# A two-layer hybrid decoder step: f16 sample products stacked over 96 rows, chunk states before exponent differences, weights split first and steps one to three places on in the retention groups

## The chip, the cores and the metric

One core of a Trainium2 chip runs the whole program. The metric is the device time of one execution in microseconds. Times are the median of three timed runs; the rows below come from one further execution that the hardware profiler recorded.

## The reference

One inference step of a decoder of two layers, for a prompt of 16 + 512 tokens and, with the same weights, for eight running sequences of four new tokens each (32 sample tokens). Every layer mixes tokens by four HGRN2 heads and four retention heads of 128 x 128 state, then runs a convolutional FFN. What bears on the change is the state update of a head, here for HGRN2 (retention is alike, with fixed decays):

```python
s_new = exp(b_last)[..., None] * s0 + einsum('bshk,bshv->bhkv', k * exp(b_last[:, None] - b), v)
```

For each sample sequence it is the old state, decayed, plus a product over its four tokens of decayed keys and values. The states of all eight sequences and of the prompt are outputs.

## The kernel before, in words

All arithmetic is f32 in effect. The large products use weights and activations split into an f16 high and an f16 low part (WH, WL, XH, XL): per 128 rows of the contraction six TensorE instructions, three products on two halves of 280 of the 560 tokens (`products`, L510). Smaller products run on f32 operands directly, where each is issued as two instructions.

A layer's mixer is nine stages. **Group** g (0 to 7) computes the four projection tiles of one head (forget gate or key, query, value, output gate; 0 to 3 HGRN, 4 to 7 retention), while TensorE also does the mixing of the head of the group before. A group has 4 tiles of 8 k-steps, 32 k-steps, and the mixing work is written into them by hand: the lists HG_SLOTS, HG_SLOTS_RT and RT_SLOTS give, for each piece of it, the k-step before which it is issued. Group 0 has no mixing work beside it; groups 1 to 3 carry HGRN heads by HG_SLOTS, group 4 the last one by HG_SLOTS_RT, groups 5 to 7 retention heads by RT_SLOTS, and the output projection the last retention head (there the slot numbers are halved, since it holds two tiles' columns of 7 k-steps). Tiles go to two accumulators in PSUM in turn: tiles 0 and 2 to accumulator 0, tiles 1 and 3 to accumulator 1, so k-step 16 needs tile 0 read out (`acc_read[0]`) and k-step 24 tile 1 (`acc_read[1]`). A scratch area SCR has two banks. Each job on a bank waits until the job before it was read (`scr_read`).

Each engine runs its own program in order, with semaphores between them.

- VectorE in an HGRN group: the score masks of the head before (`hg_scores`, L1302 on), the low half of the weight split for slot 1 (`split_lo`, L1153), the gate (`hg_gate`, L1202 to L1212, ending with a scan), the exponent differences (`hg_exponents`, L1217 to L1224), the chunk states of the head before (`hg_states`, L1342, L1347), the output gate, the keys and queries (`hg_query`), the sample states (L1300).
- VectorE in a retention group: the scores (`rt_a`, L1391), the split of slot 1, the key's rotation (L1258 to L1262), the sample states, the split of slot 0, the query's rotation, the norm of the outputs.
- ScalarE copies transposed keys and values out of SCR (`hg_a` L910 to L919, `rt_a` L960 to L970), takes the exponentials (L885 to L891), reads Q, V and G out of the accumulators (`read_acc`, L866) and does the high half of the weight split (`split_hi`, L830). In groups 1 to 3 it reads Q right behind the exponentials.
- GpSimd (POOL) spreads the sample values into VX (32 rows by 8 sequences by 128, zero where the row is another sequence's; L417), decays the old HGRN states (L423), and issues the DMAs of the states.
- SyncE issues the loads of the weights into the two halves of `stage`.

The sample products (`sample_steps`, L624) multiply the decayed keys KVTS[:, 0] by VX: two products of 32 rows by 512 columns in f32 per head, 16 heads in all.

```python
mm(SCR[:, bank, :], KVTS[:, 0, :], VX[:, 4 * n:4 * n + 4, :].rearrange("p b v -> p (b v)"), ...)   # L624
pe.wait_ge(acc_read[c], 1 + l * ACC_TILES + half_tile)          # gemm_tile, ahead of k-steps 0, 8, 16, 24
HG_SLOTS = ([1, 2, 3, 4, 5], [7, 8, 9, 10], [12, 13], [22, 22], [23, 23, 24, 24, 25, 25], [28, 28])
RT_SLOTS = ([4, 5, 6], [6, 7, 8, 9, 10], [12], [12, 13], [15, 16], [21, 22], [29])
```

The parts of RT_SLOTS are: transposes of keys, of values and of the rest; five score products; the final state; the two sample products; two output products (the second with the sample outputs, L632); two centring products; the variance. Those of HG_SLOTS are scores, transposes, chunk states, sample products, outputs, mean squares.

## Time and profile before

| | us |
|---|---|
| median of three timed runs (1738.65 to 1740.34) | 1739.92 |
| the profiled execution's own time | 1742.57 |
| its span, first to last instruction | 1741.0 |
| TensorE busy in it | 1567.8 (90%) |
| VectorE busy | 904.5 (52%) |
| ScalarE busy | 654.0 (38%) |
| GpSimd busy | 154.3 (9%) |
| mean granted TensorE clock | 0.931 of full speed |

The span holds two alike layers. In the first, groups 0 to 7 run from about 49 to 378 us, the output projection and a norm to 494, the FFN to 866; the second follows some 843 us later. The page's busy shares are means over stages of different limits, so the stage, and in it the wait that ends last, is what to look at. "L" and a number is a line of the kernel; an entry such as `[2.45 <-DVE shared L1347]` gives the idle time ahead of an instruction and what ended it.

### The profile page before, as it was taken

To read this page: it belongs to the slowest core of one execution; us is meant where nothing else is said; L and a number is where in the kernel's file an instruction comes from. 1 tells how busy PE (TensorE), PEld (TensorE's weight loads), DVE (VectorE), ACT (ScalarE), POOL (GpSimd) and SP (SyncE) were. 2 spreads that over 40 slices of the span, in tenths; PEclk is the share of its full clock that TensorE was granted. 3 is DMA by queue.
4 is the path that set the end of the run, shared out by engine and by line. 5 is a ranking of instruction groups with operands and counts; after the bars stand their busy time and mean duration, and the time that the engine had idled before them with its cause. 6 is when DMAs were issued, how large, how long until landed. Compare 5 with 4: busy or idle time off the path is not lost.

```text
span 1741.0 us, 31399 instructions
## 1 busy us (share of the span) xinstructions
PE 1567.8 (90%) x12107; PEld 1251.0 (72%) x12107; DVE 904.5 (52%) x1389; ACT 654.0 (38%) x920; POOL 154.3 (9%) x126
## 2 busy tenths in 40 slices
PE   4699999989699999999867999999886999999994
PEld 3477777767578888788755777777765888887883
DVE  4766644444565555533266665444356555553334
ACT  3645523332353334422155452333225443333213
POOL 2111111100200000000030111000002000000002
PEclk8799989988899999999978899999888999999997
DMA  6132222221123332233221224232031223322321
GB/s 192 46 90 77 75 75 75 74 74 55 57 73 97 96 96 77 70 93 95 82 66 51 74 74 111 57 88 78 27 97 48 88 83 96 96 81 74 97 66 51
DMA packets 175035, 138.05 MB, mean 79 GB/s; under 512 B 5064, under 2 KB 169192, under 8 KB 174776
## 3 DMA queue, kind: packets, MB, share of 16 engines
q1 hardware_dynamic: 168192, 113.46, 22.0%
q0 software_dynamic: 5408, 18.60, 3.8%
q10 hardware_dynamic: 1372, 5.16, 0.9%
q8 instruction: 40, 0.66, 0.2%
q14 instruction: 23, 0.19, 0.0%
HBM read 125.12 MB, written 12.07 MB: 79 GB/s over the span
## 4 chain that ended last, share of the span: by engine, by line
PE 77%; DVE 9%; ACT 6%; issue 4%; DVEq 2%; ACTq 1%; DMA 1%; SPq 0%
PE ACC L510 61%; PE SCR L624 2%; PE OT L632 2%; PE SCR L662 1%; ACT WH L830 1%; DVE X L1193 1%; PE OT L684 1%; PE SCR L545 1%; PE SCR L727 1%; DVE Z L1222 1%; DVE Fb L1206 1%; DVE WL L1153 1%; PE OT L600 1%; DVEq L1261 1%; PE OT L599 1%
## 5 line engine op out<-in xcount | busy, mean ns | idle before, releaser
L510 PE MATMUL ACC<-XH,WH 128*128 128x280 f16 x2432 | 502.6, 289 | 70.8 <-DVE XL L1196 43.1
L510 PE MATMUL ACC<-XL,WH 128*128 128x280 f16 x2432 | 502.4, 289 | 0.0
L510 PE MATMUL ACC<-XH,WL 128*128 128x280 f16 x2432 | 501.6, 289 | 0.0
L510 PEld LDWEIGHTS ACC<-XH,WH 128*128 128x128 f16 x2432 | 238.7, 101 | 153.0 <-DVE XL L1196 45.6
L1153 DVE SCALAR_TENSOR_TENSOR WL<-stage,WH 128x2048 f16<-128x2048 f32 (+1 forms) x116 | 245.9, 2120 | 182.0 <-ACT WH L830 170.2
L510 PEld LDWEIGHTS ACC<-XL,WH 128*128 128x128 f16 x2432 | 243.3, 100 | 58.6
L510 PEld LDWEIGHTS ACC<-XH,WL 128*128 128x128 f16 x2432 | 243.3, 100 | 58.0
L830 ACT ACTIVATE WH<-stage 128x2048 f16<-128x2048 f32 (+1 forms) x116 | 204.8, 1766 | 103.7 <-PE ACC L510 86.9
L510 PE MATMUL ACC<-shared,WH 128*128 128x280 f16 x1408 | 225.2, 283 | 0.2
L510 PEld LDWEIGHTS ACC<-shared,WH 128*128 128x128 f16 x1408 | 137.6, 98 | 30.8 <-issue 0.8
L510 PE MATMUL ACC<-shared,WL 128*128 128x280 f16 x704 | 141.5, 283 | 0.0
L408 POOL TENSOR_TENSOR X<-X,T 128x560 f32<-128x560 f32 x40 | 65.2, 1663 | 429.1 <-ACT T L842 429.1
L837 ACT ACTIVATE E<-X 128x560 f32 (+1 forms) x32 | 21.5, 671 | 195.5 <-DVEq L1175 195.5
L510 PE MATMUL ACC<-OHL,WH 128*128 128x280 f16 x512 | 89.0, 300 | 6.0 <-DVE X L1173 6.0
L1173 DVE SCALAR_TENSOR_TENSOR X<-ACC,X 128x560 f32 (+1 forms) x32 | 23.7, 740 | 112.1 <-PE ACC L510 111.4
L510 PEld LDWEIGHTS ACC<-shared,WL 128*128 128x128 f16 x704 | 68.9, 98 | 14.9
L1093 ACT ACTIVATE T<-ACC 128x560 f32<-128x560 f32 x44 | 28.0, 637 | 135.9 <-PE ACC L510 135.5
L510 PEld LDWEIGHTS ACC<-OHL,WH 128*128 128x128 f16 x512 | 52.3, 104 | 23.4 <-DVE X L1173 7.0
L1565 DVE SCALAR_TENSOR_TENSOR Fb<-ACC,Fb 128x560 f32<-128x560 f32 x22 | 16.3, 742 | 92.0 <-PE ACC L510 92.0
L417 POOL TENSOR_TENSOR VX<-KVTS,tab 32x1024 f32<-32x1024 f32 x16 | 30.2, 1886 | 285.4 <-ACTq L920 197.5
L510 PE MATMUL ACC<-OHL,WL 128*128 128x280 f16 x256 | 55.3, 300 | 0.0
L1548 DVE COPY AS<-T 128x32 f32<-128x32 f32 x44 | 8.0, 182 | 90.0 <-ACTq L1096 89.6
(238 smaller groups left out, 1791.4 us busy)
## 6 DMA issues: line engine op xcount, KB each, us to landing
stage<-in_w_in_dram SPq DMA_DIRECT2D x64, 512.0 KB, 5.3
stage<-in_w_a_dram SPq DMA_DIRECT2D x44, 512.0 KB, 4.3
stage<-in_w_b_dram SPq DMA_DIRECT2D x44, 512.0 KB, 4.8
stage<-in_w_down_dram SPq DMA_DIRECT2D x32, 384.0 KB, 3.3
stage<-in_w_down_dram SPq DMA_DIRECT2D x32, 320.0 KB, 3.7
out_dram<-shared POOLq DMA_DIRECT2D x16, 512.0 KB, 3.9
stage<-in_w_o_dram SPq DMA_DIRECT2D x16, 512.0 KB, 3.9
shared<-in_state_hgrn_dram POOLq DMA_DIRECT2D x8, 512.0 KB, 5.7
```

Source lines behind the costliest of these rows:

```text
L408: nc.gpsimd.tensor_tensor(X[:, m, :], X[:, m, :], MU[:, 0:T], ALU.subtract).then_inc(ln_sub, 1)
L417: nc.gpsimd.tensor_tensor(VX[:, :, :], KVTS[:, 1:2, :].to_broadcast([TS, DEC_BATCH, P]), bcast(seqm[0:TS, :], P), ALU.mult).then_inc(vx_re ...
L510: last = mm(ACC[:, acc, h, 0:HALF], lhs, x[:, xk + k, h * HALF:(h + 1) * HALF], start=begin, stop=end)
L545: last = mm(SCR[0:left.shape[1], bank, c * C // 2:(c + 1) * C // 2], left, right, start=True, stop=True)
L599: mm(o, SC[:, (c - 1) * P:c * P], QD[:, t:t + C], start=True, stop=False)
L624: mm(SCR[:, bank, :], KVTS[:, 0, :], VX[:, 4 * n:4 * n + 4, :].rearrange("p b v -> p (b v)"), start=True, stop=True).then_inc(scr_full, 1)
L632: last = mm(OT[:, 1, TP - SPLIT + DEC_SEQ * b:TP - SPLIT + DEC_SEQ * (b + 1)], S0b[:, b, :], qs[:, TP + DEC_SEQ * b:TP + DEC_SEQ * (b + 1) ...
L830: f(WH[:, s, 0:width], stage[:, s, 0:width], ACT.Copy, scale=W_SCALE).then_inc(w_hi[s], 1)
L837: f(SQT[:, 0:T], src, ACT.Square).then_inc(sq_ready, 1)
L1093: f(halves(AX[c][:, 2:2 + T]), ACC[:, c, :, 0:HALF], ACT.Copy, scale=INV_W)
L1153: stt(out=WL[:, s, 0:width], in0=stage[:, s, 0:width], scalar=W_SCALE, in1=WH[:, s, 0:width], op0=ALU.mult, op1=ALU.subtract).then_inc(w_l ...
L1173: stt(out=halves(row(m)), in0=ACC[:, c, :, 0:HALF], scalar=INV_W / ALPHA, in1=halves(row(m)), op0=ALU.mult, op1=ALU.add).then_inc(acc_read ...
```

## The change

- The sample products become one f16 product over 96 rows: keys high, high and low (KV3[:, 0], rows 0-31, 32-63, 64-95) against values high, low and high (KV3[:, 1]). The sample transposes take 96 columns, so that each block arrives in its rows; the columns are copied twice more behind K and V (`twice`). ScalarE writes all 96 rows in f16 as high parts, then a copy of the values in f32 (VTS) for the sample outputs. VectorE (`low_sample_rows`) subtracts to get the two low blocks, and only then releases SCR bank 0. POOL's VX has 96 rows in f16 and waits for the low rows (`kv_low`) instead of the copies.
- In HGRN groups VectorE runs the chunk states (`b`) ahead of the exponent differences, and the low rows behind the gate's readout.
- In retention groups (where `c` is given) VectorE does the split of slot 1 ahead of the scores; the low rows stand behind the first score job.
- RT_SLOTS moves pieces one to three k-steps on.

```diff
         AX, CX = (T1, T2), (T3, Fb)
-        VX = sb("VX", [TS, DEC_BATCH, P])
-        KVTS = sb("KVTS", [TS, 2, P])
+        VX = sb("VX", [TS3, DEC_BATCH, P], F16)
+        KV3 = sb("KV3", [TS3, 2, P], F16)
+        VTS = sb("VTS", [TS, P])
         PTS = sb("PTS", [C, TP])
...
         Fb, T1, T2, T3, B, Q, QS, QD, KE, E, V, G = (
-            sb(n, [P, T + 2]) for n in ("Fb", "T1", "T2", "T3", "B", "Q", "QS", "QD", "KE", "E", "V", "G"))
+            sb(n, [P, T + (2 * TS if n in ("KE", "V") else 2)]) for n in ("Fb", "T1", "T2", "T3", "B", "Q", "QS", "QD", "KE", "E", "V", "G"))
         at = [0]
...
         tok_ready, vx_ready, pts_ready, states_ready = sem("tok_ready"), sem("vx_ready"), sem("pts_ready"), sem("states_ready")
+        kv_high, kv_low = sem("kv_high"), sem("kv_low")
         decays_used = sem("decays_used")
...
             return ap.unsqueeze(2).to_broadcast([ap.shape[0], ap.shape[1], n])
+
+        def twice(t):
+
+            return t[:, T:T + 2 * TS].rearrange("p (a t) -> p a t", a=2)
...
-                pool.wait_ge(tok_ready, hh + 1)
-                nc.gpsimd.tensor_tensor(VX[:, :, :], KVTS[:, 1:2, :].to_broadcast([TS, DEC_BATCH, P]), bcast(seqm[0:TS, :], P),
+                pool.wait_ge(kv_low, hh + 1)
+                nc.gpsimd.tensor_tensor(VX[:, :, :], KV3[:, 1:2, :].to_broadcast([TS3, DEC_BATCH, P]), bcast(seqm[0:TS3, :], P),
                                         ALU.mult).then_inc(vx_ready, 1)
...
                         for i, src in enumerate(sources):
-                            last = nc.tensor.transpose(SCR[0:TS, bank, i * P:(i + 1) * P], src[:, TP:T], ident)
+                            last = nc.tensor.transpose(SCR[0:TS3, bank, i * P:(i + 1) * P], src[:, TP:TP + TS3], ident)
                     last.then_inc(scr_full, 1)
...
                 job(scr, bank)
-                mm(SCR[:, bank, :], KVTS[:, 0, :], VX[:, 4 * n:4 * n + 4, :].rearrange("p b v -> p (b v)"),
+                mm(SCR[:, bank, :], KV3[:, 0, :], VX[:, 4 * n:4 * n + 4, :].rearrange("p b v -> p (b v)"),
                    start=True, stop=True).then_inc(scr_full, 1)
...
                 cols_ = OT[:, 1, TP - SPLIT:REST]
-                mm(cols_, KVTS[:, 1, :], PTSS[:, :], start=True, stop=False, skip_group_check=True)
+                mm(cols_, VTS[:, :], PTSS[:, :], start=True, stop=False, skip_group_check=True)
                 for b in range(DEC_BATCH):
...
                 act.wait_ge(acc_full, 1 + tile + 1)
-                f(halves(buf[:, 0:T]), ACC[:, c, :, 0:HALF], ACT.Copy, scale=INV_W).then_inc(acc_read[c], 1)
+                last = f(halves(buf[:, 0:T]), ACC[:, c, :, 0:HALF], ACT.Copy, scale=INV_W)
+                if buf is V:
+                    last = f(twice(V), ACC[:, c, 1:2, HALF - TS:HALF].to_broadcast([P, 2, TS]), ACT.Copy, scale=INV_W)
+                last.then_inc(acc_read[c], 1)
                 if done is not None:
...
                 act.wait_ge(scr_full, full)
-                f(KVTS[:, :, :], SCR[0:TS, 0, 0:2 * P].rearrange("p (n v) -> p n v", n=2), ACT.Copy).then_inc(scr_read[0], 1)
+                f(KV3[:, :, :], SCR[0:TS3, 0, 0:2 * P].rearrange("p (n v) -> p n v", n=2), ACT.Copy)
+                f(VTS[:, :], SCR[0:TS, 0, P:2 * P], ACT.Copy).then_inc(kv_high, 1)
                 act.drain().then_inc(tok_ready, 1)
...
                 f(VTOK[0:TAIL, 4 * P:5 * P], SCR[0:TAIL, 0, P:2 * P], ACT.Copy)
-                f(KVTS[:, 0, :], SCR[0:TS, 0, 2 * P:3 * P], ACT.Copy, scale=tab[0:TS, ds(cols["k_dec_s"][0] + p, 1)])
-                f(KVTS[:, 1, :], SCR[0:TS, 0, 3 * P:4 * P], ACT.Copy).then_inc(scr_read[0], 1)
+                f(KV3[:, 0, :], SCR[0:TS3, 0, 2 * P:3 * P], ACT.Copy, scale=tab[0:TS3, ds(cols["k_dec_s"][0] + p, 1)])
+                f(KV3[:, 1, :], SCR[0:TS3, 0, 3 * P:4 * P], ACT.Copy)
+                f(VTS[:, :], SCR[0:TS, 0, 3 * P:4 * P], ACT.Copy).then_inc(kv_high, 1)
                 act.drain().then_inc(tok_ready, 1)
...
-            def hg_gate(l, p, tile):
+            def low_sample_rows(hh, at, decay):
+
+                keys, values = (slice(2 * TS, TS3), KV3[2 * TS:TS3, 0, :]), (slice(TS, 2 * TS), KV3[TS:2 * TS, 1, :])
+                dve.wait_ge(kv_high, hh + 1)
+                if decay is None:
+                    tt(keys[1], SCR[keys[0], 0, at:at + P], keys[1], ALU.subtract)
+                else:
+                    stt(out=keys[1], in0=SCR[keys[0], 0, at:at + P], scalar=tab[keys[0], ds(cols["k_dec_s"][0] + decay, 1)],
+                        in1=keys[1], op0=ALU.mult, op1=ALU.subtract)
+                tt(values[1], SCR[values[0], 0, at + P:at + 2 * P], values[1], ALU.subtract).then_inc(scr_read[0], 1)
+                dve.drain().then_inc(kv_low, 1)
+
+            def hg_gate(l, p, tile, low_rows=None):
                 n = l * HEADS + p
...
                 dve.drain().then_inc(f_ready, 1)
+                if low_rows is not None:
+                    low_rows()
...
                 tt(QD[:, 0:T], Q[:, 0:T], E[:, 0:T], ALU.mult)
+                nc.vector.tensor_copy(twice(KE), KE[:, TP:T].unsqueeze(1).to_broadcast([P, 2, TS]))
                 dve.drain().then_inc(ew_ready, 1)
...
                 for job in RT_JOBS:
+                    if job is RT_JOBS[1]:
+                        low_sample_rows(hh, 2 * P, p)
                     full, _ = scr.job(bank)
...
                 hh = l * 2 * HEADS + kind * HEADS + head
-                if a is not None:
+                if c is not None:
+                    split_lo(1, j)
                     a()
-                split_lo(1, j)
+                else:
+                    if a is not None:
+                        a()
+                    split_lo(1, j)
+                hgrn_rows = (lambda: low_sample_rows(hh - 1, 0, None)) if steps else None
                 if kind == 0:
-                    hg_gate(l, head, tile)
-                    hg_exponents(l, head)
+                    hg_gate(l, head, tile, hgrn_rows)
                     if b is not None:
                         b()
+                    hg_exponents(l, head)
                     if d is not None:
...
+                        hgrn_rows()
                         dve.wait_ge(tok_ready, hh)
...
-RT_SLOTS = ([4, 5, 6], [6, 7, 8, 9, 10], [12], [12, 13], [15, 16], [21, 22], [29])
+RT_SLOTS = ([5, 6, 9], [9, 10, 11, 12, 13], [14], [15, 16], [17, 18], [23, 24], [30])
```

## Rows read from the trace of the kernel before

**Rows 1.** The page, part 4: shares of the chain that ended last.

```profile
PE 77%; DVE 9%; ACT 6%; issue 4%; DVEq 2%; ACTq 1%; DMA 1%; SPq 0%
```

**Rows 2.** Table of stretches, group 2: engines' busy us (count), PEclk, DMA.

```profile
135.00:177.00 42.00, 39.55 (x327) 32.84 (x324) 28.79 (x52) 22.68 (x39) 6.14 (x5) 0.96 0.28 76
```

**Rows 3.** Table of waits, TensorE: us in total, times, longest.

```profile
PE SCR L624 <- DVE shared L1347: 17.7, 8, 2.5
...
PE SCR L653 <- ACT shared L960: 16.4, 6, 4.5
```

**Rows 4.** Timeline of TensorE, group 2: start, us, operation.

```profile
150.84 0.40 PE L510 MATMUL ACC<-XH,WL 128*128 128x280 f16 x2
...
153.69 2.05 PE L624 MATMUL SCR<-VX,KVTS 32*128 32x512 f32 x4 [2.45 <-DVE shared L1347]
...
159.20 0.55 PE L599 MATMUL OT<-QD,shared 128*128 128x88 f32 x2
...
170.82 0.69 PE L545 MATMUL SCR<-Z 128*44 128x44 f32 x12
```

**Rows 5.** Timeline of VectorE, group 2.

```profile
144.01 2.19 DVE L1206 TENSOR_TENSOR Fb<-Fb,T 128x560 f32<-128x560 f32 x1 [3.93 <-ACT T L877]
...
146.13 0.73 DVE L1207 TENSOR_TENSOR T<-T 128x560 f32<-128x560 f32 x1
...
148.87 0.71 DVE L1217 TENSOR_TENSOR T<-B 128x528 f32<-128x528 f32 x1
...
152.08 0.28 DVE L1342 COPY shared<-SCR 128x128 f32<-128x128 f32 x1
...
154.96 0.74 DVE L1284 TENSOR_TENSOR G<-G,shared 128x560 f32<-128x560 f32 x1 [0.40 <-issue]
```

**Rows 6.** Timeline of ScalarE, group 2.

```profile
152.19 0.67 ACT L885 ACTIVATE T<-T 128x560 f32<-128x560 f32 x1 [4.37 <-DVE DK L1224]
...
155.84 0.61 ACT L866 ACTIVATE Q<-ACC 128x560 f32<-128x560 f32 x1
```

**Rows 7.** Groups by form, ScalarE: busy, mean ns, idle before.

```profile
L970 ACT ACTIVATE KVTS<-SCR 32x128 f32<-32x128 f32 x8 | 2.0, 249 | 0.0
```

**Rows 8.** Timeline of GpSimd (POOL), group 2.

```profile
141.85 1.89 POOL L417 TENSOR_TENSOR VX<-KVTS,tab 32x1024 f32<-32x1024 f32 x1 [17.15 <-ACTq L920]
...
143.70 1.90 POOL L423 TENSOR_TENSOR shared<-shared,E 128x1024 f32<-128x1024 f32 x1
```

**Rows 9.** Timeline of VectorE in the norm stage of layer 0.

```profile
471.61 5.01 DVE L1193 TENSOR_TENSOR X<-X,QS 128x560 f32<-128x560 f32 x3 [1.78 <-ACT QS L848]
```

**Rows 10.** Table of stretches with the clock; PEclk third from the end.

```profile
302.50:306.00 3.50, 3.48 (x22) 2.47 (x23) 0.86 (x2) 1.38 (x5) 1.70 (x1) 1.00 0.00 0
...
344.00:347.25 3.25, 3.25 (x12) 1.98 (x12) 0.43 (x1) 0.92 (x4) 1.89 (x1) 0.50 0.00 0
...
385.00:391.75 6.75, 5.39 (x16) 3.26 (x17) 1.61 (x3) 2.58 (x10) 1.89 (x1) 0.50 0.01 2
...
951.50:961.75 10.25, 10.25 (x42) 7.50 (x42) 7.94 (x16) 6.00 (x9) 0.74 (x2) 0.50 0.02 7
```

**Rows 11.** Timeline of TensorE, retention groups 5 and 6.

```profile
280.44 0.40 PE L510 MATMUL ACC<-XH,WH 128*128 128x280 f16 x2
...
288.14 0.41 PE L510 MATMUL ACC<-XH,WH 128*128 128x280 f16 x2 [0.88 <-DVE T L1260]
...
302.52 0.28 PE L653 MATMUL SCR<-tab,KE 128*16 128x128 f32 x1 [1.86 <-ACT shared L960]
```

**Rows 12.** Timeline of TensorE, group 1 of both layers.

```profile
110.90 3.00 PE L624 MATMUL SCR<-VX,KVTS 32*128 32x512 f32 x4 [2.47 <-DVE shared L1347]
...
117.82 0.57 PE L599 MATMUL OT<-QD,shared 128*128 128x88 f32 x2
...
950.49 2.96 PE L624 MATMUL SCR<-VX,KVTS 32*128 32x512 f32 x4 [2.46 <-DVE shared L1347]
...
957.37 0.57 PE L599 MATMUL OT<-QD,shared 128*128 128x88 f32 x2
```

More of the change, by code:

```diff
@@ L46 @@
 T = TP + TS
+TS3 = 3 * TS
 HALF = T // 2
@@ L143, in const_tables @@
     put("mask32", causal)
-    put("seq", tok[:, None] // DEC_SEQ == np.arange(DEC_BATCH)[None, :])
+    put("seq", np.tile(tok[:, None] // DEC_SEQ == np.arange(DEC_BATCH)[None, :], (3, 1)))
     log_g = np.log1p(-np.exp2(-5.0 - np.arange(HEADS)))
@@ L154, in const_tables @@
     put("k_dec", np.where(left >= 0, np.exp(np.maximum(left, 0) * log_g[None, None, :]), 0.0) * root)
-    put("k_dec_s", np.exp((DEC_SEQ - 1 - tok % DEC_SEQ)[:, None] * log_g[None, :]) * root)
+    put("k_dec_s", np.tile(np.exp((DEC_SEQ - 1 - tok % DEC_SEQ)[:, None] * log_g[None, :]) * root, (3, 1)))
     put("gamma4", np.broadcast_to(np.exp(DEC_SEQ * log_g), (P, HEADS)))
@@ L653, in rest_transposes @@
                         nc.tensor.transpose(SCR[0:TAIL, 0, n * P:(n + 1) * P], src[:, 4 * P:TP], ident)
-                        last = nc.tensor.transpose(SCR[0:TS, 0, (2 + n) * P:(3 + n) * P], src[:, TP:T], ident)
+                        last = nc.tensor.transpose(SCR[0:TS3, 0, (2 + n) * P:(3 + n) * P], src[:, TP:TP + TS3], ident)
                     last.then_inc(scr_full, 1)
@@ L1275, in rt_query @@
                 tt(QS[:, TP:T], QD[:, TP:T], tab[:, ds(cols["q_dec"][0] + p * TS, TS)], ALU.mult)
+                nc.vector.tensor_copy(twice(KE), KE[:, TP:T].unsqueeze(1).to_broadcast([P, 2, TS]))
                 dve.drain().then_inc(ew_ready, 1)
```

## Prediction

> **What bounds the kernel now.** I read the page first: of the span of 1741.0 us the chain that ended last is 77% TensorE, 9% VectorE and 6% ScalarE [rows 1]. Then the table of stretches, to see where TensorE is not busy: in a group of a linear-recurrence (HGRN) head it is busy 39.55 of 42 us [rows 2]. So such a stage is TensorE's own work plus waits, and the table of waits names them: the sample products behind VectorE's chunk states (L624 on L1347, 17.7 us, eight times), the retention rest transposes behind ScalarE's copies (L653 on L960, 16.4 us, six times, the longest 4.5) [rows 3]; the second tile of a retention pair waits behind the rotation, L1260. Last I laid the four engines' timelines of one group side by side. The FFN stretches and the norms are not touched, and I leave them as they are.
>
> In all that follows a group has 32 k-steps, 0 to 31, each of six weight products. Group 2 of layer 0 stands for groups 1 to 3. A full-clock step is 0.715 us (three pairs, each about 0.24 after the one before, as the last pair starts at 150.84) [rows 4].
>
> **HGRN groups 1 to 3: before.** TensorE finishes step 21 at 151.24, waits 2.45 us, runs the four instructions of the two sample products in 2.05, and comes to step 24 at 159.20. The next group's step 0 is at 170.1, 0.72 before the level products at 170.82: 10.9 us after step 24 [rows 4]. VectorE ends its scan at 148.87, spends 3.21 on the exponent differences (to 152.08) and 2.88 on the chunk states (to 154.96) [rows 5]. ScalarE takes the exponentials at 152.19 and reads Q out of accumulator 1 by 156.45, 4.26 later [rows 6]. Step 24 writes accumulator 1, so it needs that readout; now it is ready 2.75 before it is asked for.
>
> **What the stacked product gives.** 32x512 f32 runs as two instructions per product, about 0.5 us each in the pace of the four; in f16 it is one instruction of 512 columns. The weight products go 280 columns in 0.12 us, so 512 cost an estimated 0.22, two of them 0.44, and 1.6 are saved per head. Bounds: nothing saved, or 1.99 less two LDWEIGHTS-bound issues of 0.1, which is 1.8.
>
> **Where it goes in groups 1 to 3.** The states now run ahead of the differences, so the wait of 2.45 goes too: bank 1 is free 1.55 us into the states, bank 0 2.49 us in. With a scan end of 149.6 (below) TensorE has both products done by about 152.4, steps 22 and 23 and the first two outputs by 154.7. But the 2.88 of states now stand ahead of the differences, and every item behind them shifts: differences, ScalarE's exponentials, Q's readout at 156.45 + 2.88 = 159.33. So step 24 waits for Q for some 5 us and starts when it did before (159.20). Both gains, 4 us a group, become a new wait.
>
> **Delay d of the scan.** The new f32 sample copy on ScalarE, 0.25 [rows 7], and two small VectorE operations (0.2 each, near the 0.28 of the 128-wide copy at 152.08 [rows 5]) put VX on POOL at about 142.6 instead of 141.85. VX and the state decay then hold POOL to 146.4 instead of 145.60 [rows 8]. L1206 took 2.19 where L1207 of equal shape took 0.73, and ended 0.6 after POOL did [rows 5, 8]; in the norm stage three VectorE operations beside POOL's took 5.01, one per POOL operation [rows 9]. So of L1206 and L1207 one now waits behind VX and one behind the decay, and L1207 ends near 147.6 instead of 146.86: d = 0.75. POOL's two rows, on 32 and on 128 partitions, agree at 1.89 and 1.90 us for 1024 elements [rows 8], so 96 partitions cost no more; there is no row for f16 on POOL. Half that time gives d = 0, one and a half times gives 1.6; I take the row's own. The Trainium skill (GPSIMD Engine Reference, section 3.1) counts about 2.6 cycles of 1.2 GHz per element for two inputs and names no type; by it VX is an estimated 2.2 us, d 1.05, and the sum 2 us higher. The row says 1.89.
>
> **Clock after the new wait.** After the wait of 4.5 the granted clock stood at 0.50 from 385.0 to 391.75, with 5.4 us of TensorE's work in it; in group 1 of layer 1 it was 0.50 for 10.25; after a wait of 1.86 it stayed at 1.00 [rows 10, 11]. TensorE's two levels, 2.4 and 1.2 GHz: work at the lower takes twice as long. I charge 4 us of half clock behind a 5.4 us wait, a loss of 2.0, bounds 0 and 3.4. The Trainium skill (TensorE: Matmul & The Clock Gate, part 1) says that the throttled state is the default and that activity releases it, and counts half of the throttled time as lost; by it alone the 5.4 us behind the wait of 4.5 would be charged, 2.7, and the sum 4 higher. The trace agrees that long waits are followed by 0.50.
>
> Groups 2 and 3 of both layers: 0.9 (readout at 160.08 for 159.20) + 2.0 = 2.9, four times, 11.6. By their sample products (110.90 and 950.49 for 153.69) group 1 lies 42.8 earlier in layer 0 and 796.8 later in layer 1, so its readout falls on 117.3 and 956.9 where step 24 stood at 117.82 and 957.37: -0.5 each. From there to the next group were 11.1 and, as the low clock ran on [rows 10], 14.5; 10.8 + 2.0 takes their place, +1.7 and -1.7 [rows 12]. Together 11.6 + 1.2 - 2.2 = **+10.6**.
>
> **Group 4** (last HGRN head beside the first retention tiles). Its order of states and key doesn't change. The key starts 0.7 later (sample copy and low rows), L1262 falls behind POOL, the states are some 0.75 late, so is the first sample product; the products then save 0.8 and 1.6 (half clock in part), and half a microsecond to 1 of half clock lies in steps that start earlier. Step 24 there follows the rotation, which follows the last output product, so this passes through: -2.2 (bounds -0.9 and -2.7), two layers, **-4.4**.
>
> **Retention groups 5 to 7.** The loop there: output products end (280.44), ScalarE copies them and splits slot 0, VectorE splits the rest and rotates, step 24 starts at 288.14: 7.70 [rows 11]. Nothing in it changes. The end of the outputs, counted from step 0, moves by two steps (1.43), by -1.7 for the products, and by 0.7 for a new wait: bank 0 is now released by VectorE's low rows, which wait for ScalarE's KV3 and VTS copies, and the second score product needs bank 0. That is +0.4 in group 5. In groups 6 and 7 the wait of 1.86 shrinks to 0.6, because the rest transposes come at step 9: -0.9 each, and group 7 loses its stretch of half clock from 344.0 to 347.25 [rows 10], -1.5. The second centre product moves behind the rotation, 0.26 in each. Together -2.1 a layer. Against it: between outputs and step 24 now lie five steps and one centre product, 4 us, instead of eight steps, so TensorE waits 2.95 for 0.88. I charge 1.0 of clock per group (bounds 0 and 1.7). Net +0.9 a layer, **+1.8**. VectorE's earlier split of slot 1 costs nothing: ScalarE's half is done 1.9 us after it begins either way, TensorE wants it at step 16, and SP's next load only starts earlier. Behind the low rows on VectorE stand the scores of the later jobs and the key rotation; the key is due at step 16 and has 0.7 to spare. POOL's VX, queued on the low rows, ends 3 us ahead of step 15.
>
> **Output projection.** The wait of 4.5 stays [rows 3], since variance (step 30) and the KTOK copies move with it; the products give 1.5, the bank wait takes 0.6, clock about as before: -0.7, twice, **-1.4**. The copies of K's and V's sample columns (0.2 each on VectorE and ScalarE) lie in gaps of 0.9 and more before the key and the variance; without that cover they cost 0.2 per head, 3 us in all.
>
> **Sum.** 10.6 - 4.4 + 1.8 - 1.4 = +6.6 on the profiled execution's 1742.57, or 1749.2; that execution is 2.65 above the median of 1739.92, so the timed runs should give 1746.5; I say 1746.
>
> **Rivals.**
> (a) The clock stays up: the falls in groups 1 to 3 came after products on 32 rows, which go, and one wait of 1.86 left it at 1.00 [rows 10]. Then 2.0 x 6 and 1.0 x 6 are not paid: 6.6 - 18 = -11.4, 1728, faster. It decides from there on whether the granted clock behind step 24 reads 1.00. Against it stands the wait of 4.5. Chance 0.25.
> (b) POOL is slower on f16 rows: VX at twice 1.89 puts d at 2.65, 1.9 more in six groups, +11.4: 1758. No row speaks for it but that none is f16. Chance 0.12.
> (c) The stacked product doesn't do what it says, and runs as long as f32: the ten heads outside groups 1 to 3 lose 1.6 each, 1762. The f16 pace of the weight products speaks against it. Chance 0.03.
> (d) VX is short (d = 0) and the clock loss is 1.0 instead of 2.0: 6.6 - 0.75 x 6 - 6 = -3.9 for both, 1736, and about 1741 where only one holds: no change. Chance 0.10.
> The forecast has 0.50, with its own 1738 to 1755.
>
> **How the numbers follow.** The range 1729 to 1759 reaches into (a) and (b). About 0.2% (3.5 us) is what a measurement can tell from no change. Faster: (a) and a little of the forecast's low end, 0.27; same: (d) and the end of the forecast near 1743, 0.18; slower: the rest, 0.55.
>
> **What would show it.** Right: in groups 1 to 3 no wait of L624 on L1347 but one of L510 on ScalarE's readout of Q, about 5 us; differences behind the states; L1206 and L1207 both long; PE clock 0.50 behind step 24; in retention groups the wait on L1260 near 3 us, the one on L960 small, a new one on the low rows near 0.7. Wrong: a group period of 39 us or less in groups 1 to 3, or Q read before TensorE asks.

## The result: slower, and the profile of the changed kernel

The changed kernel takes 1766.02 us (1765.23 to 1769.53) beside 1740.13 for the kernel before: a ratio of 1.0153, 95% interval 1.0135 to 1.0171. The forecast was 1746 with a range of 1729 to 1759, so the sign was right and the size was not: +6.6 was summed, +25.9 measured. The profiled execution took 1766.46 us with a span of 1764.9 (before: 1742.57 and 1741.0), and its mean granted clock is 0.921 for 0.931.

Stage lengths, each read from the first level products or first retention transpose of one group to those of the next. In groups 5 to 7 the transposes stand one step later in the changed kernel; its 0.715 us is taken out of group 4 and put to group 7 (in the output projection, with its halved slot numbers, they stand where they stood). The last row reaches to the next layer's first level products, or to the end:

| us, changed less before | forecast, layer 0 / 1 | measured, layer 0 / 1 |
|---|---|---|
| HGRN group 1 | +1.2 / -2.2 | +3.4 / 0.0 |
| HGRN group 2 | +2.9 / +2.9 | +7.1 / +7.1 |
| HGRN group 3 | +2.9 / +2.9 | +6.9 / +6.9 |
| group 4 | -2.2 / -2.2 | -1.5 / -1.5 |
| retention groups 5 to 7 | +0.9 / +0.9 | +1.6 / +1.5 |
| output projection and what follows | -0.7 / -0.7 | -3.7 / -3.8 |

The miss lies in groups 1 to 3. Group 1 of layer 1 took 46.9 us in both kernels; its first level products, in the kernel before and in the changed one, are these:

```profile
925.63 1.11 PE L545 MATMUL SCR<-Z 128*44 128x44 f32 x12
...
939.26 1.11 PE L552 MATMUL SCR<-Z 128*44 128x44 f32 x12
```

The waits of TensorE in the changed kernel (us in total, times, longest) answer to [rows 3]:

```profile
PE OT L606 <- ACT Q L873: 34.0, 6, 5.9
...
PE SCR L702 <- DVE T L1287: 13.9, 6, 2.9
PE SCR L660 <- ACT shared L971: 10.7, 6, 4.5
...
PE SCR L631 <- DVE shared L1375: 9.3, 14, 2.3
...
PE SCR L669 <- DVE KV L1220: 4.9, 6, 0.9
```

The first is the wait that the forecast named, at step 24 for ScalarE's readout of Q (the products' line 510 is now 517 and the outputs' 599 is 606). The second and the last are the forecast's waits behind the rotation (2.95 put down; 2.9 here in groups 5 and 6, some 1.2 in group 7) and behind the low rows (0.7 put down, 0.9 here). The waits for the sample products and the rest transposes shrank.

TensorE in group 2 of layer 0 (start, us, operation, idle before and what ended it), beside [rows 4]:

```profile
154.72 0.39 PE L631 MATMUL SCR<-VX,KV 96*128 96x512 f16 x1 [0.23 <-DVE shared L1375]
155.65 0.39 PE L631 MATMUL SCR<-VX,KV 96*128 96x512 f16 x1 [0.54 <-DVE shared L1375]
...
157.71 0.40 PE L517 MATMUL ACC<-XH,WL 128*128 128x280 f16 x2
163.66 0.73 PE L606 MATMUL OT<-QD,shared 128*128 128x88 f32 x2 [5.55 <-ACT Q L873]
...
169.20 3.58 PE L639 MATMUL OT<-QD,shared 128*128 128x4 f32 x16
...
176.59 1.11 PE L616 MATMUL SCR<-shared,tab 128*128 128x264 f32 x4
...
181.20 0.69 PE L552 MATMUL SCR<-Z 128*44 128x44 f32 x12
```

The two sample products fell from 2.05 us for both to 0.39 each, and their wait from 2.45 to 0.23 and 0.54. Then TensorE stands for 5.55, and from there to the next level products it takes 17.54 us where it took 11.62 [rows 4]. The table of stretches shows the clock over that time (busy time and count of PE, PEld, DVE, ACT, POOL; then the granted clock, third from the end; the ends of a stretch were read on a grid of 0.25 us; compare [rows 2, 10]):

```profile
132.90:181.20 48.30, 41.97 (x315) 35.09 (x314) 29.59 (x53) 22.30 (x41) 6.14 (x5) 0.86 0.31 84
157.50:162.75 5.25, 0.61 (x6) 0.26 (x3) 2.47 (x4) 3.40 (x10) 0.00 (x0) 1.00 0.04 12
162.75:176.50 13.75, 12.84 (x58) 10.87 (x59) 9.58 (x17) 6.46 (x11) 1.78 (x2) 0.50 0.20 52
176.50:181.20 4.70, 4.70 (x37) 3.60 (x34) 1.61 (x3) 1.81 (x4) 0.00 (x0) 1.00 1.06 293
```

For 13.75 us TensorE ran at the lower of its two levels, 1.2 GHz, though it was busy for 12.84 of them. Group 3, and both groups in layer 1, have the same stretch; group 1 has two shorter ones (115.0 to 121.75 and 125.25 to 128.5 in layer 0) behind a wait of 5.9.

VectorE, ScalarE and POOL in the same group, beside [rows 5, 6, 8]:

```profile
147.41 2.82 DVE L1232 TENSOR_TENSOR Fb<-Fb,T 128x560 f32<-128x560 f32 x1 [1.67 <-ACT T L887]
150.16 0.73 DVE L1233 TENSOR_TENSOR T<-T 128x560 f32<-128x560 f32 x1
...
156.03 0.71 DVE L1243 TENSOR_TENSOR T<-B 128x528 f32<-128x528 f32 x1 [0.44 <-issue]
...
163.64 0.45 DVE L1257 TENSOR_SCALAR T<-Q 128x560 f32<-128x560 f32 x1 [3.67 <-ACT Q L873]
```

```profile
159.35 0.67 ACT L895 ACTIVATE T<-T 128x560 f32<-128x560 f32 x1 [7.50 <-DVE DK L1250]
...
162.99 0.61 ACT L873 ACTIVATE Q<-ACC 128x560 f32<-128x560 f32 x1
```

```profile
145.88 1.89 POOL L424 TENSOR_TENSOR VX<-KV,tab 96x1024 f16<-96x1024 f16 x1 [17.69 <-DVEq L1221]
```

The group began 3.24 us later than in the kernel before (132.88 for 129.64). Less that, L1233 ends at 147.65 for 146.86, so the delay d is 0.79 where 0.75 was put down, and Q is ready at 160.36 where 160.08 was. POOL's f16 product on 96 partitions takes the 1.89 us of the f32 one on 32.

### The profile page after: what moved, and what is told of

It is laid out like the page before. It is cut to its first block, busy times and chain, and to the rows that moved or that the text cites. A ratio compares the mean times of both kernels' runs of the same rounds, so it can differ in the third digit from the quotient of the medians.

```text
span 1764.9 us, 31445 instructions
## 1 busy us (share of the span) xinstructions
PE 1557.0 (88%) x12075; PEld 1255.1 (71%) x12075; DVE 918.9 (52%) x1437; ACT 658.0 (37%) x952; POOL 154.3 (9%) x126
## 4 chain that ended last, share of the span: by engine, by line
PE 73%; DVE 10%; ACT 8%; issue 4%; DVEq 3%; ACTq 1%; DMA 1%; SPq 0%
PE ACC L517 60%; PE OT L639 2%; ACT WH L837 2%; DVE X L1205 1%; PE OT L691 1%; PE SCR L669 1%; PE SCR L552 1%; DVEq L1288 1%; DVE Fb L1232 1%; ACT Z L899 1%; DVE Z L1248 1%; DVE WL L1165 1%; PE OT L606 1%; DVE shared L1375 1%; PE SCR L734 1%
## 5 line engine op out<-in xcount | busy, mean ns | idle before, releaser
L517 PE MATMUL ACC<-XH,WH 128*128 128x280 f16 x2432 | 506.0, 291 | 67.5 <-DVE XL L1208 42.2
L517 PEld LDWEIGHTS ACC<-XH,WH 128*128 128x128 f16 x2432 | 241.8, 102 | 135.6 <-DVE XL L1208 45.4
L517 PEld LDWEIGHTS ACC<-shared,WL 128*128 128x128 f16 x704 | 68.9, 98 | 15.1
L424 POOL TENSOR_TENSOR VX<-KV,tab 96x1024 f16<-96x1024 f16 x16 | 30.2, 1887 | 313.3 <-DVEq L1221 313.3
```

The lines of the kernel that those rows point to most:

```text
L424: nc.gpsimd.tensor_tensor(VX[:, :, :], KV3[:, 1:2, :].to_broadcast([TS3, DEC_BATCH, P]), bcast(seqm[0:TS3, :], P), ALU.mult).then_inc(vx_r ...
L517: last = mm(ACC[:, acc, h, 0:HALF], lhs, x[:, xk + k, h * HALF:(h + 1) * HALF], start=begin, stop=end)
```

## The experiments

The theory to test: VectorE's states, placed ahead of the differences, push Q's readout back; step 24 waits; and the output products behind that wait run long at half clock. The rivals: the stacked products and their low rows themselves delay the groups; or the wait alone costs, whatever the clock. Unless a text says otherwise, an experiment is an edit of the changed kernel. "Groups" are the lengths of HGRN groups 1, 2, 3, layer 0 then layer 1, in the profiled execution; before they are 43.5, 41.2, 41.2 and 46.9, 41.2, 41.2, changed 46.9, 48.3, 48.1 and 47.0, 48.3, 48.1.

| kernel | us, median | ratio to before, 95% | groups 1 to 3, layer 0; layer 1 |
|---|---|---|---|
| states back | 1726.92 | 0.9934 [0.9916, 0.9951] | 43.6 41.3 41.3; 43.1 41.3 41.3 |
| the same again | 1728.72 | 0.9938 [0.9924, 0.9951] | 43.1 41.3 41.3; 43.6 41.3 41.2 |
| states moved alone | 1773.64 | 1.0201 [1.0184, 1.0219] | 48.2 47.5 47.7; 48.0 47.5 47.6 |
| stack alone | 1730.03 | 0.9934 [0.9909, 0.9960] | 45.5 44.3 44.3; 46.2 41.3 41.3 |
| stack and split | 1731.47 | 0.9939 [0.9917, 0.9961] | 45.4 44.3 44.3; 46.2 41.3 41.3 |
| filler ahead of the wait | 1740.13 | 1.0012 [1.0001, 1.0022] | 49.5 44.0 43.1; 46.6 44.0 43.1 |
| filler behind the wait | 1760.41 | 1.0115 [1.0098, 1.0132] | 53.8 46.4 45.4; 47.1 48.5 46.5 |
| 4-column products left out | 1737.81 | 0.9996 [0.9979, 1.0012] | 44.2 44.6 43.1; 44.2 44.6 43.1 |
| outputs ahead of the wait | 1752.38 | 1.0061 [1.0047, 1.0076] | 45.8 44.5 46.1; 45.7 44.5 46.1 |
| Q early | 1740.22 | 1.0016 [1.0001, 1.0031] | 45.4 44.4 44.4; 45.5 44.4 44.4 |
| Q and sums early | 1728.26 | 0.9936 [0.9919, 0.9952] | 47.0 41.7 41.6; 42.5 42.9 41.7 |
| and squares early | 1737.43 | 0.9993 [0.9975, 1.0010] | 42.5 45.8 42.2; 42.2 42.8 41.8 |

**States back.**

```diff
                     hg_gate(l, head, tile, hgrn_rows)
-                    if b is not None:
-                        b()
                     hg_exponents(l, head)
+                    if b is not None:
+                        b()
```

> The changed kernel with one move undone: in HGRN groups VectorE's chunk states stand behind the exponent differences again. Theory A (the order of VectorE makes the wait: with the states ahead, ScalarE's Q readout comes 2.8 us later, step 24 waits for it 5.55 us in group 2 of layer 0, and the products behind that wait run at half clock): the Q readout is back 2.8 us earlier, the wait of L606 on L873 is under 2.5 us in groups 1 to 3, less or no half clock lies behind it, and TensorE waits instead some 1 us or less for the states of bank 1. Groups 1 to 3 take 39.5 to 42 us instead of 46.9 to 48.3, total 1720 to 1735. Theory B (the low rows and the copies of the stacked product delay the whole chain of VectorE, whatever the order): groups 1 to 3 stay at 45 us or more, total 1755 or more.

Measured: 1726.92, 39 us under the changed kernel. The wait on Q is gone, and the wait for the states is back, longer than before and than the 1 us of the expectation (3.36 for 2.45 in group 2):

```profile
PE SCR L631 <- DVE shared L1375: 28.1, 14, 3.4
```

```profile
157.00:160.25 3.25, 3.25 (x18) 2.84 (x17) 2.59 (x7) 3.18 (x5) 0.51 (x1) 0.50 0.06 20
```

The low clock behind that wait is 3.25 us long, not 13.75. Groups 2 and 3 are as long as before (41.3 for 41.2): there the stacked products' gain turns into wait, as the forecast had it. Of the 15.8 us between the two profiled spans, 12.6 lie in group 4 (2.9 a layer) and in the output projection and what follows (3.4 a layer), and most of the rest in group 1 of layer 1 (43.1 for 46.9), where the low clock behind the sample products lasted 6.75 for 10.25 and did not come back. The same kernel in a second set of runs:

> The kernel with the states back behind the differences (1726.9 and, in one look each, group lengths of 41.3) once more, beside the other two on one chip. The stack alone, whose groups 1 to 3 have the same order, took 44.3 in layer 0 and 41.2 in layer 1 of one execution, with low clock from 158.5 to 165.25 and 168.75 to 172.25 in the first and 3.25 us of it in the second, and its executions ranged from 1725.5 to 1738.5. If the start of the low stretch against the end of the wait (3.4 us for the states) varies from one execution to the next, this kernel too shows executions near 1726 and near 1738; if its places of the retention steps keep it out of that, all lie within 1725 to 1729.

Its times were 1727.0 to 1729.0 and one of 1733.4: no execution near 1738, so it neither repeats the spread of the stack alone nor is quite free of one.

**States moved alone.** The kernel before with the two lines of `b()` put ahead of `hg_exponents`, nothing stacked.

> The kernel before with one move alone: VectorE's chunk states ahead of the exponent differences in HGRN groups; sample products stay f32 on 32 rows. Theory A: the wait of L624 on L1347 (2.45 us) goes, the Q readout moves from 156.45 to about 159.3 in group 2 of layer 0; the two sample products still take 2.05 us, so step 24 is asked for at about 156.8 and waits some 2.5 us. A wait of that length may or may not be followed by half clock: without it groups 1 to 3 stay near 41 to 42 and the total is 1738 to 1746; with it they take 44 to 46 and the total is 1755 to 1770. Theory B (the stacked product alone makes the loss): 1738 to 1742, granted clock 1.00 behind step 24.

```profile
PE OT L599 <- ACT Q L866: 25.2, 6, 4.2
```

```profile
163.25:177.00 13.75, 12.91 (x58) 10.88 (x59) 9.47 (x16) 6.27 (x10) 1.78 (x2) 0.50 0.20 54
177.00:181.50 4.50, 4.50 (x35) 3.63 (x34) 1.61 (x3) 1.66 (x3) 0.00 (x0) 1.00 1.09 301
```

The order alone costs 34.6 us (1773.64 less the 1739.07 of before in the same runs), more than all edits together. The wait is 4.2, not the 2.5 of the expectation, since step 24 is reached sooner; groups and total lie above the 44 to 46 and the 1755 to 1770 that were put down for half clock. The stretch of half clock is the 13.75 us of the changed kernel, here in all six groups. So the loss is neither the stack's nor in proportion to the wait.

**Stack alone.** The kernel before with stacked products; states, retention places and weight split as before. **Stack and split** adds VectorE's earlier weight split.

> The kernel before with the stacked f16 sample products alone: the order of the chunk states, the places of the retention steps and VectorE's order of the weight split are those of before. By my forecast's terms: groups 1 to 3 gain nothing, as what the products save (1.6 us) goes into the wait for VectorE's states, which also end 0.8 later (41.3 each); group 4 gains some 2.2 a layer; each retention group and the output projection gain 1 to 1.6 for the products less 0.7 for the new wait for bank 0. Total 1722 to 1734. If the stacked products themselves cost time in the HGRN groups, by the low rows or by POOL, groups 1 to 3 take 43 or more and the total is 1745 or more.

> The kernel with stacked products and the old order of the states, with the retention steps at the places of before as well; VectorE's earlier weight split stays. It differs from the stack alone by that split only and from the kernel with the states back by the places only. If the later places are what wins in the retention groups (they cut group 7 from 41.0 to 38.2 and the output projection by some 3 us, but lengthen groups 5 and 6 by 1 each), the total is 1729 to 1735, slower than the 1726.9 of the kernel with the states back. If the stacked products win there by themselves and the places only move waits, groups 5 to 7 take 37.5 to 39.5 each and the total is 1716 to 1726.

Both at 1730 and 1731, with executions from 1725 to 1738. The stack is the part that wins, some 10 us. Later places and earlier split bring nothing that these runs tell from zero: with the states back (later places) and in stack and split (places of before), retention groups 5 to 7 of layer 0 take 39.7, 42.0, 38.1 and 38.2, 40.3, 38.8, the stretch from there to layer 1's first level products 542.3 and 543.8, and from group 4's first level products to layer 1's it is 707.4 and 706.9. The 1731 of stack and split falls into the range that its expectation gave to "the later places are what wins", but the stages show that they don't.

The 44.3 us of groups 2 and 3 in layer 0 lie where the expectation put a cost of the stacked products themselves; in layer 1 the same instructions took 41.3. The trace, which is of the slowest execution, shows where the 3 us go: to the clock. In layer 0 it fell 0.4 us after the wait for the states ended (158.1) and stayed low for 6.75, then a second time for 3.5:

```profile
158.50:165.25 6.75, 6.22 (x28) 5.12 (x29) 4.65 (x11) 6.50 (x11) 0.60 (x1) 0.50 0.03 10
165.25:168.75 3.50, 3.50 (x31) 3.21 (x28) 3.20 (x8) 0.00 (x0) 0.00 (x0) 0.99 0.00 0
168.75:172.25 3.50, 3.50 (x18) 2.48 (x18) 2.88 (x3) 1.34 (x4) 1.78 (x2) 0.51 0.50 143
```

In layer 1 it fell 1.75 us after the end of the same wait (at 1001.5) and stayed low for 3.5, once. That the spread between executions (1725 to 1738) has the same reason is likely but not shown, as only one of them was profiled.

**Filler ahead of the wait.**

```diff
+                    if n == 3:
+                        for _ in range(48):
+                            mm(OT[:, 0, 300:512], WH[:, 1, 0:P], XH[:, 0, 0:212], start=True, stop=True)
```

> The changed kernel with work added, none left out: 48 more f16 products of 212 columns, into columns of the output accumulator that nothing reads, between step 23 and step 24 of HGRN groups 1 to 3. They take some 4.5 to 5 us at full clock, so TensorE works through most of the wait for Q. Theory A1 (the part that I under-sized is the half clock behind the wait): the wait of L606 shrinks to about 1 us, the granted clock behind step 24 reads 1.00, and though TensorE does more the groups fall from 48 to 42 to 43, total 1730 to 1742. Theory A2 (the long stretch behind step 24 is late for another reason, data or a queue): the clock may rise, but the groups stay at 46 us or more, total 1760 or more.

```profile
165.53 0.46 PE L606 MATMUL OT<-QD,shared 128*128 128x88 f32 x2 [1.19 <-ACT Q L876]
```

```profile
165.25:171.25 6.00, 5.72 (x48) 5.31 (x49) 4.67 (x12) 5.26 (x9) 0.00 (x0) 1.00 0.00 0
171.25:174.75 3.50, 3.50 (x15) 2.56 (x13) 3.28 (x5) 0.71 (x3) 0.90 (x1) 0.51 0.00 0
174.75:178.50 3.75, 3.75 (x31) 2.93 (x30) 3.24 (x6) 1.52 (x3) 0.89 (x1) 1.00 0.72 185
```

More work, 25.9 us less time: the wait in group 2 fell from 5.55 to 1.19 and the clock behind step 24 read 1.00. Q is as late in groups 2 and 3 as in the changed kernel, so its lateness by itself is not what cost them 7 us each; with it they take 44.0 and 43.1 for 41.2. The clock still falls once in group 2, for 3.5 us, behind the 4-column sample outputs, 5.7 us after that wait of 1.19. Groups 2 and 3 give 18.5 of the 25.4 us between the two profiled spans, groups 4 and 5 behind them 9.2. Group 1 gives nothing (49.5 and 46.6 for 46.9 and 47.0): the low clock of the stage before it lasts 11.0 and 4.9 us past its first level products, for 1.7 in the changed kernel. Why it does is not shown.

**Filler behind the wait.** Twenty of the same products as the first thing that step 24 does once Q is read.

> The changed kernel with work added, none left out: 20 more f16 products of 212 columns directly behind the wait for Q at step 24 of HGRN groups 1 to 3, ahead of the 88-column and 4-column output products that stand there. Theory C (how long the clock stays low is set by what TensorE does behind the wait: the small f32 output products keep it low, a stretch of weight-like products raises it): the filler runs at half clock, some 3.5 us, then the granted clock reads 1.00 before the outputs of step 24 are over; the low stretch is about 5 us instead of 13.75, step 24 to the next level products takes about 15 instead of 17.5, and the total is 1745 to 1758 although work is added. Theory D (the length of the wait sets it): the low stretch stays at 13 to 14 us, the filler's 3.5 us come on top of most of the rest, a group takes 50 to 51, and the total is 1775 to 1785.

```profile
171.01 3.71 PE L726 MATMUL OT<-XH,WH 128*128 128x212 f16 x20 [5.55 <-ACT Q L879]
174.52 0.60 PE L606 MATMUL OT<-QD,shared 128*128 128x88 f32 x2
```

```profile
169.00:176.00 7.00, 4.99 (x28) 4.49 (x29) 3.95 (x10) 6.21 (x10) 0.00 (x0) 0.51 0.00 0
176.00:186.50 10.50, 10.50 (x86) 8.92 (x85) 7.24 (x12) 3.03 (x8) 1.78 (x2) 1.00 0.52 138
```

The wait is the same 5.55. With 3.71 us of wide products behind it the low stretch ends after 7.0 us instead of 13.75, 5.0 us after the wait, the 4-column products run at full clock, and group 2 is 1.9 shorter with 3.71 more in it. The total, 1760.4, is 2 above the expected range, and far from the 1775 that a low stretch set by the wait alone asked for. Group 3 has 3.5 us of low clock in layer 0 and 6.75 in layer 1. In layer 1 group 2 gained nothing (48.5): a second low stretch, of 3.5 us, came behind its 4-column products. Group 1 of layer 0 is long in this kernel because the low clock of the norm stage reaches into it (to 97.5; to 87.75 in the changed kernel).

**The 4-column products left out** (what they add to the output is left out with them).

> The changed kernel without the eight 4-column f32 sample-output products (16 instructions) of each HGRN head; the samples' share from the stored states is left out of the output, all else is computed. They take 1.95 us at full clock and 3.58 at half, and stand 5.5 us behind the wait for Q. With the 5.55 us wait, the order and the 88-column output products unchanged: if the 4-column products are what holds the clock low, the low stretch behind the wait falls from 13.75 to 7 or less and groups 1 to 3 fall from 48 to 42.5 to 44, more than the 3.6 us that the products took; total 1728 to 1740. If the wait and the 88-column products hold it low by themselves, the stretch stays at 10 us or more and the groups come to 45 or more; total 1744 to 1752.

```profile
159.25:169.50 10.25, 8.62 (x38) 6.93 (x39) 7.35 (x15) 7.19 (x12) 0.36 (x1) 0.51 0.00 0
...
203.50:210.25 6.75, 4.84 (x22) 4.41 (x22) 3.80 (x9) 6.12 (x9) 0.00 (x0) 0.50 0.00 0
```

Between the two cases: 6.75 us in group 3, as in the first, 10.25 in group 2, as in the second, in both layers; the total, 1737.81, lies in the range of the first. Without the 4-column products the low stretch is shorter, and behind the wait and the 88-column products alone it is still there.

**Outputs ahead of the wait.** Their places `[23, 23, 24, 24, 25, 25]` become `[23, 23, 23, 23, 23, 23]`.

> The changed kernel with one row of numbers edited: in HGRN groups 1 to 3 all six output steps and the sample outputs stand at step 23, ahead of the wait for Q, instead of at steps 23, 24 and 25. VectorE's order is that of the changed kernel, so Q is read as late as there. Theory C (the loss is the low clock over the small output products behind the wait): some 4 us of real work fills the wait, which falls from 5.55 to about 1.5; behind it stand weight products alone, the granted clock behind step 24 reads 1.00 or is back at it within 4 us, and a group takes about 41.5, bounded by VectorE's QD; total 1720 to 1735. If the late Q by itself cost the 25 us, groups 1 to 3 stay at 45 us or more and the total at 1750 or more.

```profile
158.21 2.63 PE L639 MATMUL OT<-QD,shared 128*128 128x4 f32 x16
...
162.44 0.65 PE L517 MATMUL ACC<-XH,WH 128*128 128x280 f16 x2 [0.18 <-ACT Q L873]
```

```profile
156.00:159.25 3.25, 3.25 (x30) 3.12 (x29) 2.74 (x5) 1.13 (x4) 0.13 (x1) 1.00 0.06 20
159.25:166.00 6.75, 6.57 (x31) 4.49 (x31) 2.85 (x7) 6.61 (x12) 0.00 (x0) 0.50 0.00 0
```

The wait for Q fell to 0.18 us (group 2), and yet the clock fell in the middle of the 4-column products and stayed low for 6.75, with no wait above 0.55 us in the 10 us before. The expected 1720 to 1735 was wrong: the clock fell during these products, packed together, without a long wait ahead of them. A second wait, 2.81 us for VectorE's sample sums, opened behind. The total and two of the three groups lie where the rival put them (the late Q by itself), so this run doesn't decide against it. The filler ahead of the wait does for groups 2 and 3: there Q is as late, and they take 43 to 44.

**Q early, then what stands behind it.** ScalarE reads Q ahead of the exponentials:

```diff
-                    if d is None:
-                        read_acc(Q, 1, tile + 1, None)
+                    read_acc(Q, 1, tile + 1, None)
                     hg_exponentials(l, head)
-                    if d is not None:
-                        read_acc(Q, 1, tile + 1, None)
```

> The changed kernel with one edit on ScalarE: in HGRN groups 1 to 3 Q is read out of accumulator 1 ahead of the exponentials, as it is in the other groups, so that step 24 has its accumulator early. Theory A says that the wait at step 24 goes, but that what it waited for, the chain of VectorE's differences, ScalarE's exponentials and VectorE's query, is as late as before, so that a wait of 2 to 5 us opens where the next group asks for the query and the key; with work of full clock ahead of it, the half clock behind is shorter than 13.75 us. Groups 1 to 3 take 41 to 45, total 1735 to 1752. If the readout by itself were the whole cause, groups 1 to 3 take 38 to 40 and the total is 1705 to 1725.

Then also VectorE's sample sums ahead of its wait for the exponentials:

> The changed kernel (states ahead) with Q read ahead of the exponentials and, on VectorE, the sample sums taken out of the scratch banks ahead of the wait for the exponentials, where VectorE stood idle for 2.5 us. With Q early alone the long wait moved to the mean-square products behind these sums (L616, 6.3 us). If each of these waits is only the next one in a chain that VectorE bounds (differences, exponentials, query, weight split, QD), the L616 wait falls to about 3, bounded by ScalarE's squares, a wait for QD opens ahead of the next group's first scores, and groups 1 to 3 come to 40.5 to 42.5: total 1715 to 1730. If the banks were the whole cause, the groups take 38 to 39.5 and the total is under 1712.

Then also ScalarE's squares ahead of its weight split and query:

> A try at a kernel that beats both: states ahead, Q read and sample sums taken early as in the kernel of 1728.3, and ScalarE's squares of the output ahead of its weight split and its query sigmoid in HGRN groups 1 to 3. In that kernel the mean-square products waited 3.3 us for the squares, of which ScalarE had the input 4.9 us before it came to them. The squares delay the query by 0.7, so QD ends near 173.4 in group 2 of layer 0 and the next group's level products start by then rather than at 175.0. Groups 1 to 3 take 39.5 to 41, total 1712 to 1724. If QD is a harder bound than that (a wait of 3 us or more ahead of the level products with low clock behind), the groups stay at 41.5 and the total at 1726 to 1732.

The longest wait of TensorE in these groups moves one link on each time (kernel by kernel, from the tables of waits):

```profile
PE SCR L616 <- DVE shared L1325: 35.9, 6, 6.3
```

```profile
PE SCR L616 <- ACT shared L936: 19.5, 6, 3.7
```

```profile
173.43 0.41 PE L517 MATMUL ACC<-XH,WH 128*128 128x280 f16 x2 [2.07 <-DVE WL L1164]
```

First the mean-square products wait for the sums, then for the squares, then the next group's step 0 waits for VectorE's weight split. That VectorE's chain (states, differences, query, split, QD) sets the pace is what these waits suggest; no run shortened the chain itself. The first two came out within their expectations (1740.22 and 1728.26), and the second is as fast as the kernel with the states back. The third, 1737.43, missed its 1712 to 1724: the wait of 2.07 now stands ahead of the 44-column level products, and low clock lies over them (173.75 to 177.25 at the end of group 2, 13.75 us from 126.0 at the end of group 1); its executions range from 1732.7 to 1748.5.

## Why the forecast was wrong

- **The bound, and what VectorE's order does.** Right. The wait of the sample products became a wait at step 24 for Q, 5.55 us where some 5 was put down, and step 24 starts at 160.42 on the old scale where 160.08 was put down.
- **The stacked product.** Right: 0.39 us each from start to end, with the next instruction 0.23 behind the start where 0.22 was put down; some 10 us in all where nothing else changes (stack alone).
- **d.** Right: 0.79 for 0.75. L1232 and L1233 were not both long, as the list of signs had it: L1232 took 2.82, behind both POOL operations, and L1233 0.73. The end came out the same.
- **POOL on f16 rows, rival (b).** Out: 1.89 us. The section of the Trainium skill that the forecast cites for POOL (GPSIMD Engine Reference, section 3.1) does name a type for its measured case, f32. The measured 1.89 decides over the 2.2 that the forecast estimated from there.
- **Clock after the new wait.** This is the term that failed. It charged 4 us of half clock, a loss of 2.0, with 3.4 as the upper bound. In groups 2 and 3 of both layers the stretch was 13.75 and the loss 5.7 to 5.9 (17.54 less 11.62 in group 2 of layer 0). In group 1 it is 15.1 from the end of the wait to the next level products, where 13.5 was put down (10.8 + 2.0, and the 0.72 from step 0 to the level products). Over the six groups that is 4 x 3.8 + 2 x 1.6 = 18.4 us too little. Between the profiled executions the miss is 17.3 (23.9 less 6.6): these 18.4, 2.5 for a step 24 that came later than put down (0.3 in groups 2 and 3, 0.6 in group 1), 1.3 in group 4 and 1.4 in the retention groups, less 6.1 in the output projections and what follows, to within 0.2. The size was taken from rows that follow waits of like length [rows 10], though the longest of them, 10.25 us in group 1 of layer 1, was already far over the 4 that was charged, and no row asked what stood behind the wait. Behind this one stand output products of 88 and of 4 columns; with wide products put first in that place the same wait is followed by a shorter low stretch.
- **Group 1 of layer 1**, -2.2 put down, came to 0.0. One low clock took the place of another: behind the new wait of 5.95 stand stretches of 6.75 and 3.5 us, where 10.25 and 3.25 stood before.
- **The rule of the Trainium skill** (TensorE: Matmul & The Clock Gate, part 1), half of the throttled time as lost: the trace agrees. Half of the 12.84 us that TensorE was busy at the lower clock is 6.4, where 5.9 was lost. It is the throttled time that the forecast had wrong, not what it costs. That activity releases the throttle, as the same part says, needs the row beside it: TensorE was busy for 12.84 of 13.75 us and the clock stayed at 0.50.
- **Retention groups.** +1.6 and +1.5 a layer for +0.9, and near only because the parts cancel: +2.6, +1.2 and -2.2 for groups 5, 6 and 7 of layer 0, where the terms give +1.7, +0.4 and -1.1. The wait behind the rotation is 2.9 in groups 5 and 6, with 3.5 us of half clock behind each.
- **Group 4** came to -1.5 for -2.2, within its bounds of -0.9 to -2.7. **The output projection** and what follows gave 3.7 a layer where 0.7 was put down. The wait for bank 0 (0.6) does not occur there: its six times are those of groups 5 to 7. The half clock behind the wait of 4.5 lasted 3.5 us (405.0 to 408.5) for 6.75 [rows 10], and a later one 13.75 (429.0 to 442.5) for 17. "Clock about as before" failed there too, but it is not all: with the states back the first of these stretches is 6.75 again and the stage still gives 3.4.
- **Rival (a)**, the clock stays up, gave 1728. That is the time of the kernel with the states back, for another reason: there the wait for Q is not made.

What stays open: why, behind one and the same wait, the clock falls 0.4 us after its end in one layer and 1.75 after it in the other, why the low stretch without the 4-column products is 10.25 us in group 2 and 6.75 in group 3, and why in the changed kernel it is 13.75 in groups 2 and 3 but 6.75 and 3.5 in group 1. The runs show that the loss is half clock behind the wait and that it changes with the work put there; they don't give its length beforehand.

## What to carry to other kernels

In these runs a moved wait cost itself and, on top, what the work behind its new place lost at half clock, so ask what stands there. Behind the wait for Q, with the small output products first, TensorE ran at half clock for 13.75 us in groups 2 and 3, and with twenty wide products first for 3.5 to 10.25; behind the wait for the states, with the sample products and weight products first, for 3.5 to 10.25. Of the two orders of VectorE the one that waits there is 39 us faster, though it too waits 3.4 us in each group. The versions that beat both kernels by more than the noise include the stacked products without the move of the states: 0.9934 and 0.9938 of the time before in two sets of runs.

## What the runs showed of the hardware that was not expected

- A busy TensorE stayed at the lower clock: 12.84 us of TensorE's work in a stretch of 13.75 ran at 0.50 throughout ([rows 10] had 10.25 of 10.25 already), and the kernel with the states moved alone shows the same 13.75 behind a shorter wait of 4.2.
- The clock fell without a wait ahead: from 1.00 to 0.50 at 159.25, in the middle of sixteen f32 instructions of 4 columns, with TensorE busy 3.25 of the 3.25 us before (outputs ahead of the wait).
- The same instructions with the same wait cost 3 us more or less by where the clock falls (44.3 and 41.3 in two layers of one execution). Executions of that kernel lie up to 13 us apart, so parts worth a few us could not be told apart here.
- POOL's product of 1024 elements takes 1.89 us with f32 on 32 partitions and with f16 on 96.
